# Six stages of transformer blocks on one core: the passages from one stage to the next

## The reference, cut to what matters

```
for s in 0..5:                              # D = 1024
    h = x * rsqrt(mean(x^2) + 1e-6) * gain * (1 + scale_s) + shift_s
    y = mixer_s(h)                          # ends in a product with a weight matrix
    x = x + gate_s * (y * rsqrt(mean(y^2) + 1e-6) * gain')
# mixers: 0 attention, 1 swiglu, 2 differential attention, 3 swiglu,
#         4 conformer convolution module, 5 swiglu with a 3-tap convolution
# shift, scale, gate: six vectors of 1024 a layer, from silu(c) @ ada_w + ada_b
```

## Time and profile before

| | us |
|---|---|
| median of 3 runs | 1045.06 |
| lowest, highest | 1042.86, 1047.76 |
| the profiled execution's own time | 1044.48 |
| its span | 1042.7 |
| PE, DVE, ACT, POOL busy | 971.0, 844.6, 542.9, 69.6 |
| mean granted TensorE clock | 0.958 |

### The profile page before, as it was taken

How to read it: one execution, slowest core, us unless ns; L and a number is a source line. 1 busy time by engine, 2 the same in 40 slices (tenths; PEclk the granted TensorE clock), 3 DMA queues, 4 the chain that set the end, 5 groups by cost and what they waited for, 6 DMA issues and landing times.

```text
span 1042.7 us, 19826 instructions
## 1 busy us (share of the span) xinstructions
PE 971.0 (93%) x6740; PEld 894.1 (86%) x6740; DVE 844.6 (81%) x1354; ACT 542.9 (52%) x1013; POOL 69.6 (7%) x126
## 2 busy tenths in 40 slices
PE   3899988999999898997999999989997989999997
PEld 2899967999999797995899999979995789999995
DVE  6779988788888787776788888879997789987875
ACT  2464445444444456664544444459996455555452
POOL 3100012000000201113100000020000010000001
PEclk9899998999999899998899999989997989999998
DMA  9999983999999765561499999982330548666630
GB/s 338 325 330 317 318 266 111 332 316 311 310 313 312 222 186 167 162 201 40 147 337 309 310 310 311 310 263 82 94 109 0 153 136 279 212 187 182 182 120 40
DMA packets 259077, 233.39 MB, mean 224 GB/s; under 512 B 7513, under 2 KB 208986, under 8 KB 259034
## 3 DMA queue, kind: packets, MB, share of 16 engines
q1 hardware_dynamic: 256256, 226.52, 71.3%
q0 software_dynamic: 1536, 4.81, 1.3%
q10 hardware_dynamic: 1242, 1.51, 0.4%
HBM read 231.75 MB, written 1.06 MB: 223 GB/s over the span
## 4 chain that ended last, share of the span: by engine, by line
PE 68%; DVE 16%; issue 6%; ACT 3%; DMA 3%; SPq 2%; POOL 1%; DVEq 0%; POOLq 0%; ACTq 0%
PE work L476 39%; PE Y L489 21%; DVE wlo L1131 4%; DVE acc L1143 3%; DMA ada_raw<-in_ada_w 3%; DVE mix L1508 3%; SPq L248 2%; PE work L538 2%; PE work L649 2%; PE work L512 1%; DVE mix L1234 1%; ACT whi L837 1%; PE Y L752 1%; ACT work L901 1%; ACT xs L925 1%
## 5 line engine op out<-in xcount | busy, mean ns | idle before, releaser
L1131 DVE TENSOR_TENSOR wlo<-raw,whi 128x1024 fp32r<-128x1024 f32 x286 | 347.3, 1222 | 91.2 <-ACT whi L837 90.2
L476 PE MATMUL work<-h_hi,whi 128*128 128x256 f32 x1440 | 408.7, 284 | 12.7 <-DVE h_lo L1191 12.4
L476 PE MATMUL work<-h_lo,whi 128*128 128x256 f32 x1440 | 405.8, 282 | 0.0
L476 PE MATMUL work<-h_hi,wlo 128*128 128x256 f32 x1440 | 405.7, 282 | 0.0
L837 ACT ACTIVATE whi<-raw 128x1024 fp32r<-128x1024 f32 x286 | 298.5, 1055 | 134.5 <-PE work L476 66.4
L476 PEld LDWEIGHTS work<-h_hi,whi 128*128 128x128 f32 x1440 | 274.6, 191 | 18.3 <-issue 14.6
L476 PEld LDWEIGHTS work<-h_lo,whi 128*128 128x128 f32 x1440 | 274.1, 190 | 3.1
L476 PEld LDWEIGHTS work<-h_hi,wlo 128*128 128x128 f32 x1440 | 274.9, 191 | 0.0
L1143 DVE SCALAR_TENSOR_TENSOR acc<-ada_raw,csil,acc 128x512 f32 (+1 forms) x256 | 191.3, 747 | 5.4 <-DMA ada_raw<-in_ada_w 3.1
L489 PE MATMUL Y<-whi,ab_hi 128*128 128x512 f32 x328 | 105.9, 404 | 1.9 <-DVE ab_lo L1251 1.9
L489 PE MATMUL Y<-wlo,ab_hi 128*128 128x512 f32 x328 | 103.1, 395 | 0.0
(11 more groups left out here) (187 smaller groups left out, 1145.6 us busy)
## 6 DMA issues: line engine op xcount, KB each, us to landing
ada_raw<-in_ada_w SPq DMA_DIRECT2D x88, 512.0 KB, 6.9
raw<-in_ffn_w_in SPq DMA_DIRECT2D x88, 512.0 KB, 7.4
ada_raw<-in_mod_w SPq DMA_DIRECT2D x48, 512.0 KB, 6.5
raw<-in_ffn_w_out SPq DMA_DIRECT2D x44, 512.0 KB, 5.2
raw<-in_f_up_w SPq DMA_DIRECT2D x44, 512.0 KB, 4.0
raw<-in_moba_w_qkv SPq DMA_DIRECT2D x24, 512.0 KB, 7.8
raw<-in_diff_w_qkv SPq DMA_DIRECT2D x24, 512.0 KB, 4.8
raw<-in_a_pw_w SPq DMA_DIRECT2D x24, 512.0 KB, 5.7
```

The source lines that it names most:

```text
L476: mm = pe.matmul(dst, w[:, u, ws], h[:, k, :], start=(k == 0 and m == 0), stop=(k == KT - 1 and m == 2))
L1131: dve.tensor_tensor(wlo[:, u, :], raw[:, u, :], whi[:, u, :].bitcast(F32), ALU.subtract).then_inc(lo[u], 1)
```

## The change

It is made of these edits.

1. `row_product` is built from `row_tile`, one row tile of a unit, with its own wait for `wlo`. The last one of a stage goes bank by bank: three matmuls for f = 0, then three for f = 1, and a semaphore for each bank (`y_done`). In stages 1, 3 and 5 the last two units go in the order (unit 0, tile 0), gate vector, (unit 1, tile 0), (unit 0, tile 1), (unit 1, tile 1), with PE's last step written out of the loop. In stage 4 the last four units go for tile 0 and then for tile 1.
2. In the last step of stages 1 and 3 ACT makes `a_hi` and DVE `a_lo` ahead of their work on the next weight unit.
3. `post_norm`: DVE multiplies in place in PSUM, in the order f = 0, 1, each behind its bank's square; it forms the sum of the two halves and eps itself (a 128x1 instruction), so that POOL has only the power left. Tile 0 is updated before tile 1 is multiplied. L1240 reads y from PSUM.
4. `pre_norm`, for all stages but the first: x is transposed into eight banks, one block to each, those of `Y` too. Blocks 0 and 1 are scaled, split and released to PE one by one, the others in pairs; the blocks are shared 0, 1, 3, 4, 7 to DVE and 2, 5, 6 to ACT. The columns of scale and shift go to work[3], the gate vector of the odd stages to work[0:2], and their waits move with them. DVE copies the columns between its two scalings of x.
5. POOL clears `acc` and loads the gains behind the split of h also at the start of stages 2 and 4. In stage 5 the sums for the gate vector start one step later, and the first step works on the next weights only after its `a_lo`.

```diff
-GATE_BANK = {0: 1, 1: 2, 2: 2, 3: 2, 4: 2, 5: 2}
+GATE_BANK = {0: 1, 1: 0, 2: 2, 3: 0, 4: 2, 5: 0}
-            end = n - 1 if s == LAST else n
+            end = n - 1 if s % 2 else n
@@ POOL
-                pool.tensor_scalar(msy[:, c], ssy[:, 2 * t:2 * t + 1], EPS, None, ALU.add).then_inc(msy_done, 1)
...
-                pool.tensor_tensor(msy2[:, c], msy[:, c], ssy[:, 2 * t + 1:2 * t + 2], ALU.add).then_inc(msy2_done, 1)
-                pool.wait_ge(msy2_done, n + 1)
-                pool.tensor_tensor(rsy[:, c], msy2[:, c], mhalf, ALU.pow).then_inc(rsy_done, 1)
+                pool.wait_ge(msy_done, 2 * s + t + 1)
+                pool.tensor_tensor(rsy[:, c], msy[:, c], mhalf, ALU.pow).then_inc(rsy_done, 1)
...
                     pool.wait_ge(mod_gf, s // 2)
+                    pool.wait_ge(hlo, h_parts_before(s + 1))
                     acc_init(s + 2, s // 2, 5 * D, 6 * D)
@@ PE
+            def row_tile(a_h, a_l, u, n, t, first=False, end=False):
                 pe.wait_ge(lo[u], n + 1)
...
+                if end:
+                    for f in range(2):
+                        for m, (a, w) in enumerate(parts):
+                            mm = pe.matmul(Y[:, 2 * t + f, :], a[:, ts], w[:, u, f * 512:(f + 1) * 512],
+                                           start=False, stop=(m == 2))
+                        mm.then_inc(*((used[u], 1) if t and f else (y_done, 1)))
...
+                products(NI_F - 1, 1)
+                last_down(0, 0)
+                pe.wait_ge(act_done, fb + FT - 1)
                 mod_gate_f(s // 2)
-                down(NI_F - 1, 1, end=True)
+                last_down(1, 0)
+                last_down(0, 1)
+                last_down(1, 1)
...
+                        if s and t == 0 and k == KT - 1:
+                            pe.wait_ge(mod_cols_used, s + 1)
+                        mm = pe.transpose(x_bank(s, k)[:, t * P:(t + 1) * P], xs[:, t, k * P:(k + 1) * P], ident[:])
+                        if t == TT - 1:
                             mm.then_inc(hT, 1)
@@ ACT, pre_norm
+                    high(0, 1, 1, 0)
+                    scaled(2)
+                    high(1, 2, 2, 0)
+                    high(2, 4, 3, 1)
+                    scaled(5)
+                    high(4, 6, 4, 2)
+                    scaled(6)
+                    high(6, 8, 5, 3)
@@ DVE, pre_norm
+                    scaled(0)
+                    scaled(1)
+                    low(0, 1, 1)
+                    scaled(3)
+                    low(1, 2, 2)
+                    scaled(4)
+                    low(2, 4, 3)
+                    scaled(7)
+                    low(4, 6, 4)
+                    low(6, 8, 5)
@@ DVE, post_norm
-                    for f in (1, 0):
+                    for f in range(2):
                         b, fs = 2 * t + f, slice(f * 512, (f + 1) * 512)
-                        if f == 0:
-                            dve.wait_ge(ssy_done, 4 * s + b + 1)
-                        dve.tensor_tensor(yG[:, t, fs], Y[:, b, :], G[:, fs], ALU.mult).then_inc(y_tmp, 1)
-                for t in range(TT):
+                        dve.wait_ge(ssy_done, 4 * s + b + 1)
+                        if f:
+                            dve.scalar_tensor_tensor(msy[:, t:t + 1], ssy[:, b - 1:b], EPS, ssy[:, b:b + 1], ALU.add,
+                                                     ALU.add).then_inc(msy_done, 1)
+                        dve.tensor_tensor(Y[:, b, :], Y[:, b, :], G[:, fs], ALU.mult).then_inc(y_tmp, 1)
                     dve.wait_ge(y_tmp, 4 * s + 2 * t + 2)
                     dve.wait_ge(rsy_done, 2 * s + t + 1)
-                    dve.scalar_tensor_tensor(xt[:, t, :], yG[:, t, :], rsy[:, t:t + 1], xt[:, t, :], ALU.mult,
+                    yG = Y[:, 2 * t:2 * t + 2, :].rearrange("p f n -> p (f n)")
+                    dve.scalar_tensor_tensor(xt[:, t, :], yG, rsy[:, t:t + 1], xt[:, t, :], ALU.mult,
                                              ALU.add).then_inc(x_ready, 1)
```

More of the change, by code:

```diff
@@ L1032, in step @@
                             prep(j, i + (nb + 1))
-                    if more:
+                    last = isinstance(i, int) and i == NI_F - 1 and j == 1
+                    if more and not last:
                         prep(2 + j, i + (nb + 1))
@@ L1037, in step @@
                     act.activation(a_hi[:, j, :], act32[:, j, :], ACT.Copy).then_inc(ahi, 1)
+                    if more and last:
+                        prep(2 + j, i + (nb + 1))
                 def both(i, more):
@@ L1389, in sums, with low @@
                             gemv_step(s // 2 + 1, i - 2, 4 * j + q)
+                    def low():
+                        dve.wait_ge(ahi, i * 2 + (rb + j + 1))
+                        dve.wait_ge(act_done, F + 1)
+                        dve.tensor_tensor(a_lo[:, j, :], act32[:, j, :], a_hi[:, j, :].bitcast(F32),
+                                          ALU.subtract).then_inc(alo, 1)
+                    last = isinstance(i, int) and i == NI_F - 1 and j == 1
                     if s == 5:
@@ L1406, in step @@
                                                  ALU.mult, ALU.add).then_inc(cv_seq, 1)
-                        if more:
+                        lead = start and j == 0
+                        if more and not lead:
                             prep(j, i + (nb + 1))
@@ L1436, in step @@
                                           ALU.mult).then_inc(act_done, 1)
+                        if last:
+                            low()
                         if more:
@@ L1439, in step @@
                         sums(3)
-                    dve.wait_ge(ahi, i * 2 + (rb + j + 1))
-                    dve.wait_ge(act_done, F + 1)
-                    dve.tensor_tensor(a_lo[:, j, :], act32[:, j, :], a_hi[:, j, :].bitcast(F32),
-                                      ALU.subtract).then_inc(alo, 1)
+                    if s == 5 or not last:
+                        low()
+                    if s == 5 and lead:
+                        prep(j, i + (nb + 1))
+                        prep(2 + j, i + (nb + 1))
                 def both(i, more):
@@ L1557, in _ @@
             for s in range(LAST + 1):
-                columns(s)
                 pre_norm(s)
```

203 lines of the change are left out of this document (110 added, 93 removed).

## The result

The changed kernel takes 1034.3 us (median of four runs, 1031.5 to 1034.9); the kernel before, beside it, 1045.95. The ratio is 0.9892 (95% interval 0.9871 to 0.9913). Forecast were 1030.7 and a range of 1024 to 1039. In the profiled execution the time is 1034.28 and the span 1032.5, 10.2 less than before.

A forecast was written before the change was run, and what follows sets the result against it. PE, busy 93% of the span, bounds the kernel, with slackless chains in the passages and at the end. 7.2 + 5.3 - 0.2 + 1.9 = 14.2 us off 1044.5 gives 1030.3; forecast 1030.7, range 1024 to 1039.

The forecast's parts named there:

- Step A: From the last output products to tile 1's transposes in five passages: the transposes start earlier, 7.2 us in all.
- Step B: From tile 1's transposes to the first column product's end: no gain at full clock, 5.3 us from earlier clock return.
- Step C: The kernel's end: tile 1's update of x starts earlier after the last output product, gaining 1.9 us.
- Inside the stages: Row products: the added middle wait costs nothing, and PE-bound stages pass on what a passage gains.
- Rival 1: Column products of all passages: clock returns late everywhere, 4.7 us less gain, 1035.4, or about 1040; chance 20%.
- Rival 2: In `pre_norm`: tighter hand-overs or shorter ACT parts, last rest at s + 5.2 (s: tile 1's transposes start), 1027; chance 20%.
- Rival 3: Middle of the passage chain: not shortened, PSUM multiplications at 0.9 or power still blocked, 1034 to 1038; chance 10%.
- Rival 4: In 90 row products: the added middle wait holds up PE's queue, 1061 at 0.34 us each; chance 4%.

The follow-up runs named there:

- the second profile: The changed kernel run and profiled once more with no edit; 1032.5 us, 0.9883 of the kernel before.
- The filled passages of before: The kernel before with extra matmuls by a tile of zeros in its passages, nothing of the change; 1042.6 us, 0.9975 of before.

## Why the prediction was right

**Step A** (earlier transposes of tile 1): forecast 0.9, 1.7, 0.9, 1.7, 2.0 = 7.2. Their start, behind the last output product: 6.9, 6.1, 6.9, 6.1, 5.6 us, before 7.8 to 8.0. Gains 0.9, 1.9, 0.9, 1.9, 2.2 = 7.8. The walk through passage 1 holds step by step: with 0.56 for the later end of stage 0 taken off, the updates start at 153.45 and 156.13 (forecast 153.45, 156.12), the scaling of tile 0 at 157.33 (157.32), that of tile 1 ends at 160.02 (160.0). Passages 2, 4 and 5 are each 0.2 better. The multiplication in PSUM is 0.69, the small sum 0.15, as taken. The order with PSUM and sum does this without the eight banks (7.2); the order alone gives 4.1 of it, held back in four passages by the copies of the columns, and how the rest divides is open.

**Step B** (split and clock): forecast 0, 1.4, 2.5, 0, 1.4 = 5.3. The passages' gains less A: -0.1, 1.2, 2.4, -0.1, 1.2 = 4.6. (For passage 3 the forecast's own numbers, 2.7 less 0.35, give 2.35 and not 2.5.) PE starts 2.2 us behind tile 1's first transpose (forecast 2.0), the last rest ends at 6.1 (5.9), the product at 7.0 (6.7). In this profile the clock was back within 5.3 us of the first transpose in all five, as taken. That it came back so early in every one is in part luck: in the second profile passage 4 took 9.5 us. That this gain is the clock's was argued then. The two kernels with and without the eight banks now show it, by passage: the eight banks gain where the clock was late and nothing where it was not. The filled passages of before bear it out.

**Step C** (the end): forecast 1.9, measured 1.84. Tile 1's update starts 1.65 behind the last output product, forecast 1.55.

**Inside the stages**: "PE-bound stages pass on what a passage gains" held in stages 1 and 3 to 0.01 us. Stages 4 and 5 went -0.3 and +0.2. For stage 2 I had 0.2 given back. It is the term that was mis-sized: 3.6 in the first profile and 0.2 in the second, and no more than 0.6 when the clock is held in both kernels. I had read stage 2's idle stretches as waits of one chain and not as places where the clock can fall; the earlier trace rows shows that mechanism, and I applied it to passages only.

**The rivals.** Rival 1 (clock late everywhere) did not come, but single passages have it: passage 4 of the second profile took 16.8 and not 16.0, passage 3 with y in SBUF 17.6 and not 16.7. Here is passage 4 of the second profile, PE's stretches with the clock, whose first column product started at 689.7:

```profile
691.00:692.00 1.00, 0.96 (x4) 0.66 (x4) 1.00 (x3) 0.91 (x3) 0.00 (x0) 0.50 0.00 0
...
694.00:695.00 1.00, 1.00 (x6) 1.00 (x6) 1.00 (x1) 1.00 (x2) 0.71 (x2) 0.50 0.00 0
695.00:696.00 1.00, 1.00 (x10) 1.00 (x9) 1.00 (x2) 0.73 (x2) 1.00 (x2) 0.90 0.00 0
```

It costs 0.8 there; rival 1 gave 0.9. Rival 2 (tighter hand-overs) fell: the last rest ends at 6.1, not 5.2. Rival 3 fell for this kernel; its blocking exists in one passage with y in SBUF, and in all five of before (1.21 to 1.23 for the power). Rival 4 (the wait amid each row product) fell: stages 1 and 3 have their length to 0.01 us.

## What to carry to other kernels

Where a pass over two tiles ends a stage, finish one tile's products first: the second tile's products then hide the first's chain, and that was 7.9 of 14.2 us by itself, part of it through the clock. Cut before and after at the same marks and compare piece by piece: the gains were where the sum had put them to half a microsecond, and the shortfall sat in one stage that the change hardly touches. Before a single profile is made the base of a forecast, list where the granted clock is below 1.00, and count each such place as a few us of luck; filling a wait with idle matmuls paid here in stage 2, and cost time in the passages, where work that another engine waits for stands behind them.

## What the runs showed of the hardware

- The same code differs in time by where the clock falls. The changed kernel's stage 2 took 121.6 us in one profile and 118.1 in another, with the clock at 0.72 and 0.86 over the same 12 us of it. Of the runs of before, eight with a mean clock of 0.953 took 1046.6 to 1047.7 us, ten at 0.966 to 0.967 took 1042.2 to 1044.2. But those at 0.961 took 1041.1 to 1046.5, so the mean clock alone does not give the time; it matters where the clock falls.
- A busy TensorE can run at the lower level: 2.00 of 2.00 us busy and a clock of 0.50, with small column products and 256-column fillers. Fillers in the passages held the clock through some of them and not through others, with either width: 20 of 256 columns in three of five, 28 of them in two, 17 of 512 columns, in the kernel before, in three.
- A GpSimd power of 0.55 us took 1.53 when it met a VectorE update with both inputs in SBUF, and 0.55 beside the same update with one in PSUM. Started 0.13 us ahead of an update with both inputs in SBUF it took 0.54, and the update 1.29, as when alone. Started 0.14 us behind a VectorE scaling with its one tensor input in SBUF it took 1.02.
